# Prompt attention: GpSimd takes the low parts of the sixteen diagonal probability blocks of a head, VectorE those of the twenty-four full blocks, in place of every fourth step on GpSimd

## The reference, cut to what matters

```python
logits = jnp.einsum('bqhd,bkhd->bhqk', qblk, k, preferred_element_type=jnp.float32) * scale
logits = logits + cblk.swapaxes(1, 2)[..., None] - ck_t[:, :, None, :]
mask = k_pos[None, :] <= pblk[:, None]
logits = jnp.where(mask, logits, -jnp.inf)
probs = jax.nn.softmax(logits, axis=-1)
return jnp.einsum('bhqk,bkhd->bqhd', probs.astype(v.dtype), v)
```

## Time and profile before

| | |
|---|---|
| median of 3 runs | 2313.01 us (2310.67 to 2316.7) |
| span of the profiled execution, first to last instruction | 2309.7 us |
| mean granted TensorE clock | 0.953 of full speed |
| prompt attention, first to last probability block | about 1318 to 1793 us of the span |
| TensorE, VectorE, ScalarE, GpSimd busy in the whole span | 89%, 34%, 29%, 23% |

### The profile page before, as it was taken

How to read it: one execution, slowest core, us unless ns; L and a number is a source line. 1 busy time by engine, 2 the same in 40 slices (tenths; PEclk the granted TensorE clock), 3 DMA queues, 4 the chain that set the end, 5 groups by cost and what they waited for, 6 DMA issues and landing times. The chain is left out here.

```text
span 2309.7 us, 29897 instructions
## 1 busy us (share of the span) xinstructions
PE 2057.3 (89%) x10448; PEld 1879.9 (81%) x10448; DVE 788.6 (34%) x1223; ACT 680.6 (29%) x1210; POOL 531.7 (23%) x350
## 2 busy tenths in 40 slices
PE   3569999999999999999999698898998368997998
PEld 2569999999999999999999476666776258996886
DVE  7522122131111000000000687787887331223554
ACT  4331111113232111111111166666677230002221
POOL 6501111010000101011010124444445222420322
PEclk9979999999999999999999699999999679998999
DMA  6211120124444222121121826665651519645442
GB/s 229 98 35 30 45 72 18 55 71 130 140 132 130 101 85 94 63 75 70 72 72 48 176 47 129 129 129 120 128 111 42 167 64 367 222 155 184 155 140 85
DMA packets 194501, 254.85 MB, mean 110 GB/s; under 512 B 58313, under 2 KB 162905, under 8 KB 189241
## 3 DMA queue, kind: packets, MB, share of 16 engines
q1 hardware_dynamic: 194441, 254.14, 37.8%
HBM read 155.51 MB, written 98.45 MB: 110 GB/s over the span
## 5 line engine op out<-in xcount | busy, mean ns | idle before, releaser
L481 PE MATMUL pr_bank<-hT_hi,w_hi 128*128 128x416 f32 x960 | 342.7, 357 | 9.2 <-SPq L306 9.2
L482 PE MATMUL pr_bank<-hT_lo,w_hi 128*128 128x416 f32 x960 | 339.7, 354 | 0.0
L483 PE MATMUL pr_bank<-hT_hi,w_lo 128*128 128x416 f32 x960 | 339.4, 354 | 0.0
L481 PE MATMUL pr_bank<-hT_hi,pr_w_hi 128*128 128x416 f32 x960 | 338.7, 353 | 0.0
L483 PE MATMUL pr_bank<-hT_hi,pr_w_lo 128*128 128x416 f32 x960 | 336.3, 350 | 0.0
L482 PE MATMUL pr_bank<-hT_lo,pr_w_hi 128*128 128x416 f32 x960 | 336.2, 350 | 0.0
L1207 DVE TENSOR_TENSOR at_p_lo<-at_p,at_p_hi 128x512 fp32r<-128x512 f32 (+2 forms) x240 | 201.5, 845 | 82.5 <-ACT at_p_hi L1157 81.7
L1156 ACT ACTIVATE at_p<-at_s 128x512 f32<-128x512 f32 (+1 forms) x320 | 170.6, 533 | 117.5 <-PE at_s L1077 61.2
L707 ACT ACTIVATE pr_out_a<-pr_bank 128x416 f32<-128x416 f32 (+1 forms) x140 | 72.4, 517 | 430.0 <-PE pr_bank L483 430.0
L481 PEld LDWEIGHTS pr_bank<-hT_hi,w_hi 128*128 128x128 f32 x960 | 182.7, 190 | 11.6 <-POOLq L688 9.3
L686 POOL TENSOR_TENSOR pr_w_lo<-pr_w,pr_w_hi 128x1024 fp32r<-128x1024 f32 x24 | 60.8, 2535 | 541.1 <-ACT pr_w_hi L699 490.5
(11 more groups left out here) (250 smaller groups left out, 3496.0 us busy)
## 6 DMA issues: line engine op xcount, KB each, us to landing
merge_gates<-pr_out_a SPq DMA_DIRECT2D x80, 208.0 KB
mg_gates<-merge_gates SPq DMA_DIRECT2D x40, 416.0 KB, 3.9
w<-w_tiles SPq DMA_DIRECT2D x24, 512.0 KB, 3.4
pr_w<-w_tiles SPq DMA_DIRECT2D x24, 512.0 KB, 3.6
mixed<-mg_mixed SPq DMA_DIRECT2D x40, 208.0 KB, 2.9
ln_x<-x_prompt SPq DMA_DIRECT2D x16, 512.0 KB, 3.7
h_rows<-ln_h SPq DMA_DIRECT2D x16, 512.0 KB, 2.9
at_qs<-q_hi SPq DMA_DIRECT2D x16, 512.0 KB
```

The lines of the kernel that those rows point to most:

```text
L481: pe.matmul(out, w_hi, x_hi, start=(i == 0), stop=False)
L482: pe.matmul(out, w_hi, x_lo, start=False, stop=False)
L483: last = pe.matmul(out, w_lo, x_hi, start=False, stop=(i == len(parts) - 1))
```

## The change: who makes which low part

Before, the step number alone decides. After, `on_pool[st]` is true for the 16 diagonal steps; GpSimd makes their low parts and VectorE those of the 24 full steps. The counts that `low_value` hands to TensorE follow. Nothing else is changed: the same instructions with the same operands, on another engine.

```diff
-        POOLS = 4
+        on_pool = [kb >= 4 * q for q, kb in steps]
+        per_pool = sum(on_pool)
...
         def low_value(h, st):
-            if st % POOLS == POOLS - 1:
-                return lo_pool, NS // POOLS * h + st // POOLS + 1
-            return lo_dve, (NS - NS // POOLS) * h + st - st // POOLS + 1
+            before = sum(on_pool[:st])
+            if on_pool[st]:
+                return lo_pool, per_pool * h + before + 1
+            return lo_dve, (NS - per_pool) * h + st - before + 1
...
             def low(h, st):
-                if st % POOLS == POOLS - 1:
+                if on_pool[st]:
                     return
...
                 for st in range(NS):
-                    if st % POOLS == POOLS - 1:
+                    if on_pool[st]:
                         low(h, st)
                     if before and st in FINISH_LOW:
                         lower(h - 1, 1 - b, FINISH_LOW[st])
```

## The result

| | before | after |
|---|---|---|
| median (11 runs each) | 2310.67 us (2308.21 to 2316.7) | 2319.69 us (2312.33 to 2323.55) |
| ratio to before, 95% interval | | 1.0036 [1.0025, 1.0046] |
| span of the profiled execution | 2309.7 us | 2315.3 us (2315.1 forecast) |
| mean granted TensorE clock | 0.953 | 0.950 |

The account below looks back on a forecast made before the run. Bound by TensorE in head 0, transfers (steps 9 to 31) then TensorE in heads 1 to 5, GpSimd and VectorE in head 7; 1.3 + 0.6 + 0 + 1.5 + 2.5 - 0.5 = +5.4 us, 2313.0 to 2318.4, range 2310 to 2326.

Parts of the forecast that it names:

- Steps 9 to 31 of heads 1 to 5, 0: Transfers set the pace there; ScalarE's 6.77 us wait covers `upper` of q = 0 coming 1.4 us later: no cost.
- as I had set for a sign: In heads 1 to 5, ScalarE's wait at `upper` of q = 2 stays at 5 to 8 us.
- The operations: GpSimd's low parts take 1.27, 1.00, 0.73 and 0.46 us by width, 13.8 us per head instead of 9.5.
- The passage, 0.18 us each: Between heads, seven times, GpSimd's step 0 comes slightly late: +1.3 us in all; bounds 0 and 0.9 each.
- the 0.5 from which I called the passage mis-sized: Inverses stay about 62 us apart; spacing growing by more than 0.5 us would mean the passage was mis-sized.
- the first rival: GpSimd late in every passage between heads, about 1.0 us each, adding 5.7 us: 2324 us; chance 0.34.
- The loops, 0: GpSimd's loop turns, ahead of a low part TensorE soon needs: 0 to 2.4 us, taken as 0.
- Heads 6 and 7, +1.5 and +2.5: Head 6: VectorE's row maxima later, +1.5 us; head 7: GpSimd and VectorE bind, taking turns of 1.70 us, +2.5 us.
- a bound below: Head 6: if GpSimd's lighter load gives turns back, the lower bound is -1 us.
- the 1.4 that I set for a sign: VectorE's full low parts in head 7 average about 1.4 us or more.
- Head 0, +0.6: First step of head 0: nothing hides GpSimd's 1.27 us in place of 0.68; bounds 0 and 0.6.
- given back, -0.5: TensorE's short waits for unit maxima in heads 0 and 6: a third of 1.5 us is saved.

Follow-up runs that it names:

- Taking about half of the cover away: Changed kernel, VectorE's inverse at step 6 instead of 9: 2290.57 us; also with ScalarE's and VectorE's loops written out and the last head's old assignment: 2283.43 us.
- the run with both repairs: Changed kernel with ScalarE's and VectorE's heads 2 to 5 written out and the assignment of before in the last head: 2309.34 us, 0.9997.
- head 7 repaired: Changed kernel with the assignment of before (every fourth step on GpSimd) in the last head alone: 2314.34 us, 1.0025.
- three steps: Kernel before with VectorE's inverse at step 6 instead of step 9: 2285.9 us, 0.9894.
- a fourth step: Kernel before with VectorE's inverse at step 5 instead of step 9: 2292.63 us, 0.992.
- the late `lower`: Changed kernel with GpSimd's last `lower` of a head (q = 3) behind the low part of step 39 instead of step 37: 2318.2 us, 1.0035.

## Why the prediction was right, and where it was off

**Steps 9 to 31 of heads 1 to 5, 0: right, and shown.** `upper` of q = 0 in head 3 comes 16.6 us behind the inverse, not 14.7: 1.9 us later where I said 1.4. `upper` of q = 2 comes 35.2 behind it, not 35.05. The later start is swallowed, and the wait of 6.8 to 8.3 us is still there, as I had set for a sign. Taking about half of the cover away did not bring it out; with none left it was not tried.

**The operations: right.** GpSimd's groups by shape (behind the bar the busy time in us and the mean of one in ns), against 1.27, 1.00, 0.73 and 0.46 us:

```profile
L1295 POOL TENSOR_TENSOR at_p_lo<-at_p,at_p_hi 128x512 fp32r<-128x512 f32 x32 | 41.1, 1284 | 231.4 <-ACT at_p_hi L1159 231.4
...
L1295 POOL TENSOR_TENSOR at_p_lo<-at_p,at_p_hi 128x384 fp32r<-128x384 f32 x32 | 34.0, 1064 | 4.3 <-ACT at_p_hi L1159 3.4
L1295 POOL TENSOR_TENSOR at_p_lo<-at_p,at_p_hi 128x256 fp32r<-128x256 f32 x32 | 23.4, 733 | 0.1
L1295 POOL TENSOR_TENSOR at_p_lo<-at_p,at_p_hi 128x128 fp32r<-128x128 f32 x32 | 14.7, 459 | 2.2 <-ACT at_p_hi L1159 2.2
```

**The passage, 0.18 us each: right in kind.** Four passages cost 0 to 1.0 us, 0.4 on average, within the bound of 0.9 but for the last 0.1. In heads 4 and 5 the inverses lie 1.0 and 0.6 us further apart than before, over the 0.5 from which I called the passage mis-sized; in heads 1 and 2 they do not. No wait for GpSimd shows in them, so the first rival (1.0 us in every passage) falls, and the run with both repairs, where all passages but the last are as changed, excludes it.

**The loops, 0: a term that was too small.** I asked only what GpSimd's turn costs, and wrote that the one into head 4 "lies beside ScalarE's"; what ScalarE's and VectorE's loops would cost behind the change stood in no term. The turn into head 4 is the passage where ScalarE's exponentials come latest: p_hi of step 0 is ready at 1561.4, and GpSimd's 1.27 us in place of VectorE's 0.68 follow on it directly. TensorE stands 2.25 us in place of 1.80. In the profiled execution the lower clock behind it makes that 4.8 us; the three other profiles with such a stand show 0.8 to 1.0 us between the inverses of heads 3 and 4, so 4.8 is not the usual price. By the ratios writing out ScalarE's and VectorE's loops is worth 4 us in the changed kernel (1.0036 to 1.0019), 6.5 with head 7 repaired (1.0025 to 0.9997) and 3 with step 0 alone on GpSimd, each with an uncertainty of about 4, and nothing in the kernel before. The Trainium skill (Runtime: NRT & Kernel Launch, Instruction fetch mechanics) says that a taken branch to code outside the two pages that an engine holds stalls it until the target is fetched. The 3.14 us of ScalarE, 0.85 without the loop, agree with that; the page gives no duration, and no run here shows the fetch itself.

**Heads 6 and 7, +1.5 and +2.5: head 7 right, head 6 wrong.** Between inverses the two take 96.8 us against 95.05, +1.7; the single values there, -2.4 and +4.1, only say that the inverse that divides them came earlier. The first exponential of head 7 divides them better (before, then after; the row of TensorE is its wait at `turn` in head 6):

```profile
1743.91 0.60 ACT L1156 ACTIVATE at_p<-at_s 128x512 f32<-128x512 f32 x1 [0.85 <-PE at_s L1079]
```

```profile
1739.71 0.28 PE L1116 MATMUL at_m<-at_eye,at_neg_max 128*32 128x128 f32 x1 [1.22 <-DVE at_neg_max L1227]
...
1749.09 0.60 ACT L1158 ACTIVATE at_p<-at_s 128x512 f32<-128x512 f32 x1 [0.85 <-PE at_s L1081]
```

From there to the last inverse head 7 takes 54.7 us against 52.3, +2.3 where I said +2.5; with the assignment of before in it, 52.6. Head 6, from its own first exponential on, takes 58.3 us against 58.6, -0.3 where I said +1.5: TensorE's wait at `turn`, which I expected to grow from 2.21 us, fell to 1.22. VectorE is done with the row maxima earlier, which I had only as a bound below. In head 7 the first `upper` comes 1.8 us later behind that exponential (1.4 forecast), the `upper`s then take 17.2 us where they took 17.9, and the end 1.2 us more (1.3 to 1.9 forecast). While both engines have work, they go in turns of 1.70 us, as predicted. But the turns end near 1792 us: VectorE's full low parts average 1.10 us between the two inverses, not the 1.4 that I set for a sign.

```profile
L1209 DVE TENSOR_TENSOR at_p_lo<-at_p,at_p_hi 128x512 fp32r<-128x512 f32 x21 | 22.3, 1098 | 13.2 <-ACT at_p_hi L1159 13.1
```

The Trainium skill (SBUF — State Buffer, Who interferes with whom) has VectorE with two SBUF inputs and GpSimd's reads block each other; GpSimd's 1.73 in place of 1.29 us while they go in turns agree.

**Head 0, +0.6, and given back, -0.5: not shown.** The 1.25 us by which head 0 is longer lie beside a longer time at the lower clock. TensorE's waits for unit maxima fall from 6.5 to 2.7 us; in heads 1 to 5 the transfers hide what that gives.

So the sum came near by luck: in the profiled executions the passage into head 4 cost 4.8 us where my terms had 0.2, while heads 6 and 7 cost about 2 us where they had 4.

**What stays open.** That the loops and the last head make the loss is shown by the run that repairs both; which operation loses the time at the loops, and how, is not settled. Moving only step 0 costs 0.28%, yet moving all but step 0 costs 0.36%, so the effects do not add up, and one profile for each kernel cannot show how often the clock falls. Of four profiles in which TensorE stood 2.23 to 2.27 us there, it fell behind the stand in one. The runs give indications only: the mean granted clock is 0.9500 over the 11 runs of the changed kernel and 0.9527 over 81 runs of the kernel before on the chips of the experiments, and within one kernel's runs 0.001 of clock goes with 1.2 to 1.9 us. By that some 4 of the 8 us come from lower clocks somewhere in the span. But writing the loops out does not raise that mean (0.9504 against 0.9500 in the changed kernel, 0.9512 against 0.9516 with the last head repaired), and yet those kernels are the faster, so what it saves does not look like clock.

## What to carry to other kernels

Ask of each place separately what hides a moved operation: here the same move was free in twenty-odd steps a head, because transfers set the pace, and it cost something only at the loops and in the last head, where nothing hides it. When work is moved between engines, look at the program's irregular places (loop turns, first and last iterations) before the regular ones. And when a stall proves to be a chain of transfers, start the chain earlier: three steps bought 1.1% with one number, a fourth step bought nothing more.

## What the runs showed of the hardware

A stand of TensorE of about 2 us can cost more than itself (seen in one profile): behind the one of 2.25 us the granted clock was 0.52 for 10 us, and the same 123 matmuls took 4.4 us more; but three other profiles with a stand of the same length at that place show no fall. At the stands of 4.0 to 5.2 us in heads 1 to 5 of the kernel before the clock fell each time, to 0.5 for 6.8 us. When a written-out program replaced its loop, ScalarE's idle time at the turn fell from 3.14 to 0.85 us. VectorE's own turn shows as 2.41 us of "issue" time in the changed kernel and as 1.9 to 3.0 us in three of its variants with the loop (step 0 back on VectorE, the late `lower`, the last head repaired), though in the kernel before, and with step 0 alone on GpSimd, it shows none at that place; why, no run tells. The stage also begins at the lower clock for a time that differs from execution to execution (5.5 us of head 0 before, 8.8 in the changed kernel, 14.6 with its loops written out); up to the first exponential of head 1, head 0 takes 55.1, 56.1 and 58.7 us in these three.
